# An encoder layer on one core: in each attention step the next head's turned piece moves ahead of the turned probabilities

## Chip, cores and metric

The kernel runs on one core of one Trainium2 chip. The metric is the device time of one execution in microseconds (us).

## What is computed

One encoder layer in float32 for 1024 tokens (prompt) and 256 tokens (sample), which share the weights. The attention of the 8 heads is the part that the change touches:

```
q = norm(c_q) @ w_uq ; kv = norm(c_kv) @ w_ukv          # 8 heads
q, k = norm(q), norm(k), rotary on the last 64 of 192 channels
s = einsum('bqhd,bkhd->bhqk', q, k) * 192**-0.5         # bidirectional
p = softmax(s) ; o = einsum('bhqk,bkhd->bqhd', p, v) ; o @ w_b_out
```

Ahead of it stand the input projection, a gated spatial mixing and its projection; behind it the projection of `o`, the output projection and a layer of 16 experts which each choose their tokens. Every matrix product runs as three products of high and low parts ("hi" and "lo"), to keep float32 precision.

## The kernel before

Five engines run programs of their own, each in its written order, and semaphores tie them together. There are 10 chunks of 128 query tokens, 8 of the prompt (1024 keys) and 2 of the sample (256 keys). The attention stage goes through 80 steps: step n works on head h = n // 10 and on chunk ORD[s], s = n % 10, with ORD = (0, 1, 2, 3, 8, 9, 4, 5, 6, 7). So the steps s = 4 and s = 5 are the small ones. The stage is a pipeline by hand. In step n

- PE (TensorE) issues `scores(n)`, ten matmuls of 512 columns (five of 256 in a small step); `turn_prob(n - 2)`, 8 (or 2) transposes of the probabilities of step n - 2, L1414; one half of `values`, 12 matmuls of 256 columns (3 if the pair of chunks is the small one), L419 to L421, for the pair whose first step is n - 4 or n - 5; and `turn_head`, L1342, 4 or 2 transposes that turn one of nine pieces of the next head's queries and keys out of the token-major tile `tok`. Steps s = 0 to 8 turn one piece each, step s = 9 and head 7 turn none. Pieces 0 to 2 are q, 3 to 5 k, 6 to 8 the rotary parts of both; their sizes are 4, 4 and 2 blocks.
- ACT (ScalarE) does `high(n - 2)` (L2045, pt_hi out of the turned probabilities), `expo(n)` (L2055), at odd n `out_pair` (L2062, which takes the values out of PSUM), and `high_head` (L2011, or L2014 to L2017 for a rotary piece) on the turned piece.
- DVE (VectorE) does `top(n)` (L2540, L2542: the maximum and the bias of the exponential), `low(n - 2)` (L2549, pt_lo), `inverse(n)` (L2555) and `low_head` (L2498, or L2503 and L2505) on the turned piece.
- POOL (GpSimd) scales the probabilities of step n (L984), and in step s = 4 it splits the next head's values (L974, L976).
- SP (SyncE) stores the values and, behind the last turn of a head, loads the queries (L724) and keys (L727) of the head after the next into `tok`.

Pieces of heads 1 to 7 all go through one PSUM bank (`x_bank` gives 7), and the turned probabilities through another pair of banks. What `turn_head` and `turn_prob` wait for:

```
pe.wait_ge(S["q_in"], 16 * (H // 2 + h + 1))
...
free = x - 1 if h == 0 else x
...
if free > 0:
    pe.wait_ge(S["x_hi"], free)
    pe.wait_ge(S["x_lo"], free)
```

```
pe.wait_ge(S["norm_pool"], n + 1)
if n > 0:
    pe.wait_ge(S["pt_lo_dve"], n)
```

`x_hi` counts the pieces whose high part ACT has made, `x_lo` those whose low part DVE has made. A turn of piece x (x counts through all heads) starts when both count x, that is when the piece before has left the bank. `scores(n)` waits for the exponential of step n - 2.

Of the kernel before, what the change touches and what calls it, by code (L numbers as in the profile page):

```python
# [33 lines left out]
H = 8  # L34
# [30 lines left out]
def block_no(p, i):  # L65

    return 8 * (p - 1) + i
# [27 lines left out]
def split_no(g):  # L95

    return g + 1 if g < 2 else g - 1
# [4 lines left out]
PIECES = 9  # L102
# [24 lines left out]
def piece(x):  # L127

    return (0, 2, 1)[x // 3], 4 * (x % 3), (4, 4, 2)[x % 3]
# [26 lines left out]
def build(nc, x_p, x_s, norm1_g, w_in, v_norm_g, w_spatial, b_spatial, w_a_out, q_norm_g, w_uq,  # L156
# [3 lines left out]
    with ctx:  # L160
# [28 lines left out]
        def lin_set(j, b):  # L189
            o = 3 * BANK * j + BLOCKS[b][0]  # L190
            return PS[:, o:o + BLOCKS[b][1]]
# [143 lines left out]
        with ExitStack() as s:  # L335
# [3 lines left out]
            with ExitStack() as s2:  # L339
                sb(s2, "act_room", [P, 2, KD, T])  # L340
                s = s2
# [4 lines left out]
            with ExitStack() as s2:  # L346
                s = s2
# [59 lines left out]
        def at(name, n):  # L407

            return n + credit.get(name, 0)
# [7 lines left out]
        def mm3(pe, out, lh, ll, rh, rl, first, last):  # L417

            pe.matmul(out, lh, rh, start=first, stop=False)  # L419
            pe.matmul(out, lh, rl, start=False, stop=False)  # L420
            return pe.matmul(out, ll, rh, start=False, stop=last)  # L421
# [128 lines left out]
        def x_bank(x):  # L550
            return bank(6 + x % 2 if x < PIECES else 7)
# [544 lines left out]
        def _(pe):  # L1096
# [194 lines left out]
            for p in range(1, PAIRS):  # L1291
                one, other = banks(p)
                for i in range(8):
                    n = block_no(p, i)
# [33 lines left out]
            def turn_head(x):  # L1328

                h, i = divmod(x, PIECES)  # L1330
                kind, c0, cn = piece(i)
                pe.wait_ge(S["q_in"], 16 * (H // 2 + h + 1))
                if kind > 0:
                    pe.wait_ge(S["kv_in"], 16 * (H // 2 + h + 1))
                free = x - 1 if h == 0 else x
                if h == 0:
                    pe.wait_ge(S["pa_copy"], UNITS)
# [3 lines that stand above are left out]
                for c in range(cn):  # L1341
                    last = pe.transpose(x_bank(x)[:, c * P:(c + 1) * P],  # L1342
                                        tok[:, c0 + c, (0, NOPE, HEAD + ROPE)[kind]:][:, 0:P], ident[:])
                last.then_inc(S["x_pe"], 1)
# [39 lines left out]
            def scores(n):  # L1384
                h, s = divmod(n, NCH)
                hd, c = heads[h % 2], ORD[s]
                k0, kn = keys(c)
                if s == 0:
                    if h < 2:
                        pe.wait_ge(S["consts_dve"], 2 * GRP + h + 1)  # L1390
                    pe.wait_ge(S["x_hi"], PIECES * (h + 1))
                    pe.wait_ge(S["x_lo"], PIECES * (h + 1))
                if n > 1:
                    pe.wait_ge(S["exp_act"], n - 1)
                else:
                    pe.wait_ge(S["evac"], 3 * G_B - (3 if n == 0 else 0))
                q = slice(c * P, (c + 1) * P)
                for o in range(0, kn, BANK):
                    w = min(BANK, kn - o)
                    out, k = bank(s_bank(n) + o // BANK, w), slice(k0 + o, k0 + o + w)  # L1400
                    pe.matmul(out, hd["q_hi"][:, q], hd["k_hi"][:, k], start=True, stop=False)  # L1401
                    pe.matmul(out, hd["q_hi"][:, q], hd["k_lo"][:, k], start=False, stop=False)  # L1402
                    pe.matmul(out, hd["q_lo"][:, q], hd["k_hi"][:, k], start=False, stop=False)
                    pe.matmul(out, hd["qr2"][:, q], hd["kr2"][:, k], start=False, stop=False)
                    last = pe.matmul(out, hd["qr2"][:, q], hd["krl"][:, k], start=False, stop=True)  # L1405
                last.then_inc(S["scores_pe"], 1)

            def turn_prob(n):
                kn = keys(ORD[n % NCH])[1]
# [3 lines that stand above are left out]
                for k in range(kn // P):  # L1413
                    last = pe.transpose(bank(4, kn)[:, k * P:(k + 1) * P], prob[:, n % 3, k * P:(k + 1) * P], ident[:])  # L1414
                last.then_inc(S["probT_pe"], 1)

            def values(pr, half):
                h = pr // 5
                hd = heads[h % 2]
                k0, kn = keys(ORD[2 * (pr % 5)])  # L1420
                ks = kn // P // 2
                if half == 0:
                    pe.wait_ge(S["pt_lo_dve"], 2 * pr + 2)
                    if pr % 5 == 0:
                        pe.wait_ge(S["v_lo_pool"], h + 1)
                    if pr > 0:
                        pe.wait_ge(S["values_act"], pr)
                for k in range(half * ks, (half + 1) * ks):
                    v = slice(k0 + k * P, k0 + (k + 1) * P)
                    last = mm3(pe, bank(6, 2 * P), hd["v_hi"][:, v], hd["v_lo"][:, v], pt_hi[:, pr % 2, k],  # L1430
                               pt_lo[:, pr % 2, k], k == 0, k == 2 * ks - 1)
                if half:
                    last.then_inc(S["values_pe"], 1)

            def b_row(j, k, bs=(0, 1, 2)):

                if k == 0:
                    if 0 in bs:
                        pe.wait_ge(S["w_split"], split_no(G_B + j))
                    pe.wait_ge(S["exp_act"], STEPS if 2 in bs else STEPS - 1)  # L1440
                    if j == 1:
                        pe.wait_ge(S["pt_lo_dve"], STEPS)
                if 0 in bs:
                    pe.wait_ge(S["part_lo"], at("part_lo", KD + k + 1))
                for b in bs:
                    t0, tn = BLOCKS[b]
                    last = mm3(pe, lin_set(j, b), w_hi[:, j, k], w_lo[:, j, k], o_hl[:, k, 0, t0:t0 + tn],
                               o_hl[:, k, 1, t0:t0 + tn], k == 0, k == KD - 1)
                    if k == KD - 1:
                        last.then_inc(S["tile_pe"], 1)  # L1450

            for n in range(STEPS + 4):
                h, s = divmod(n, NCH)
                if n < STEPS:
                    scores(n)
                if n == STEPS:
                    for k in range(2):
                        b_row(0, k, (0, 1))
                if 2 <= n < STEPS + 2:
                    turn_prob(n - 2)  # L1460
                if n >= 4:
                    values((n - 4) // 2, n % 2)
                if h < H - 1 and s < PIECES:
                    turn_head(PIECES * (h + 1) + s)
                if n == STEPS:
                    for k in range(2):
                        b_row(0, k, (2,))
                elif STEPS < n < STEPS + 3:
                    b_row(0, n - STEPS + 1)
# [1399 lines left out]
```

## Time and profile before

| | |
|---|---|
| median of 3 runs | 2082.37 us (2081.34 to 2083.27) |
| profiled execution | 2082.28 us, span 2080.6 us |
| PE busy | 2036.2 us, 98% of the span |
| DVE, ACT, POOL busy | 1351.8, 955.2 and 903.4 us |
| mean granted clock of PE | 0.994 |
| attention stage | 713.9 to about 1065 us |

The span runs from the first to the last instruction. Busy times say how long an engine had an instruction in it, and matmuls overlap, so that PE counts as busy through waits that are shorter than the tail of a matmul. The start times in the timeline say more.

### The profile page before, as it was taken

How to read it: one execution, taken by the hardware profiler on the slowest of the kernel's cores; microseconds unless marked ns; L12 is line 12 of the kernel's file. 1: busy time of each engine (PE TensorE's matmuls, PEld its weight loads, DVE VectorE, ACT ScalarE, POOL GpSimd, SP SyncE). 2: the span in 40 equal slices, each digit the busy share in tenths (PEclk: the TensorE clock that was granted, in tenths of full speed). 3: DMA queues.
4: the chain of work that ended last, by engine and by line, in shares of the span. 5: the costliest groups of instructions: out<-in, count | busy, mean ns of one | idle time of the engine just before them, and what ended most of it. 6: DMA issues, size and time to landing. Idle time of an engine off the chain costs nothing.

```text
span 2080.6 us, 33247 instructions
## 1 busy us (share of the span) xinstructions
PE 2036.2 (98%) x13266; PEld 1685.5 (81%) x13266; DVE 1351.8 (65%) x1629; ACT 955.2 (46%) x1188; POOL 903.4 (43%) x640
## 2 busy tenths in 40 slices
PE   8999999999999999999999999799999999999997
PEld 8888888888789888888888877677777777777775
DVE  7864455456767477777655348966777767767774
ACT  8112211113555366666631033456566555655663
POOL 0975555566655376666632601412222322222221
PEclk9999999999999999999999999999999999999999
DMA  4223444333677622232134432588888778888873
GB/s 153 104 104 133 163 166 144 118 92 127 240 234 248 222 64 87 80 104 67 54 112 157 159 142 82 222 343 316 317 308 301 277 276 315 316 316 315 303 286 107
DMA packets 168938, 398.98 MB, mean 192 GB/s; under 512 B 16513, under 2 KB 88193, under 8 KB 168833
## 3 DMA queue, kind: packets, MB, share of 16 engines
q1 hardware_dynamic: 154096, 344.43, 45.2%
q0 software_dynamic: 7680, 20.98, 4.5%
q10 hardware_dynamic: 7056, 32.12, 4.4%
q8 instruction: 72, 1.18, 0.2%
q14 instruction: 34, 0.27, 0.0%
HBM read 318.19 MB, written 79.30 MB: 191 GB/s over the span
## 4 chain that ended last, share of the span: by engine, by line
PE 83%; DVE 10%; ACT 3%; POOL 2%; issue 1%; DMA 1%; SPq 0%; DVEq 0%; POOLq 0%; ACTq 0%
PE PS L1629 25%; PE PS L419 13%; PE PS L420 13%; PE PS L421 13%; PE PS L1660 8%; PE PS L1414 2%; DVE small L2540 2%; DVE topi L2667 1%; DVE topv L2665 1%; DVE work L2669 1%; ACT prob L2055 1%; PE PS L1401 1%; PE PS L1342 1%; PE PS L1405 1%; PE PS L1402 1%
## 5 line engine op out<-in xcount | busy, mean ns | idle before, releaser
L419 PE MATMUL PS<-act_hi,w_hi 128*128 128x256 f32 (+1 forms) x800 | 275.7, 345 | 6.5 <-POOL w_lo L881 2.8
L420 PE MATMUL PS<-act_lo,w_hi 128*128 128x256 f32 (+1 forms) x800 | 270.3, 338 | 0.0
L421 PE MATMUL PS<-act_hi,w_lo 128*128 128x256 f32 (+1 forms) x800 | 269.9, 337 | 0.0
L984 POOL TENSOR_SCALAR prob<-prob,small 128x1024 f32<-128x1024 f32 (+1 forms) x80 | 200.4, 2505 | 120.9 <-DVE small L2555 120.9
L1054 POOL DMA_INDIRECT y_s<-ob_s,ixs_s x16 | 43.9, 2742 | 346.4 <-DVE ob_s L2827 346.4
L2772 DVE TENSOR_TENSOR elo<-raw,ehi 128x2048 fp32r<-128x2048 f32 x65 | 148.7, 2289 | 39.5 <-ACT ehi L2157 39.5
L419 PEld LDWEIGHTS PS<-act_hi,w_hi 128*128 128x128 f32 x800 | 151.9, 190 | 24.1 <-POOL w_lo L881 3.1
L421 PEld LDWEIGHTS PS<-act_hi,w_lo 128*128 128x128 f32 x800 | 151.6, 190 | 16.4
L1629 PE MATMUL PS<-ehi,xT_hi 128*128 128x512 f32 x520 | 164.0, 397 | 0.7 <-DVE xT_lo L2740 0.4
L420 PEld LDWEIGHTS PS<-act_lo,w_hi 128*128 128x128 f32 x800 | 152.0, 190 | 14.7 <-issue 0.7
L1629 PE MATMUL PS<-elo,xT_hi 128*128 128x512 f32 x520 | 160.6, 390 | 0.0
L1629 PE MATMUL PS<-ehi,xT_lo 128*128 128x512 f32 x520 | 160.4, 390 | 0.0
L2157 ACT ACTIVATE ehi<-raw 128x2048 fp32r<-128x2048 f32 x68 | 129.9, 1913 | 63.9 <-PE PS L1629 54.7
L1906 ACT ACTIVATE stg<-stg 128x512 f32<-128x512 f32 x60 | 37.4, 632 | 253.9 <-DVE stg L2321 253.9
L1629 PEld LDWEIGHTS PS<-elo,xT_hi 128*128 128x128 f32 x520 | 97.6, 188 | 20.7
L1629 PEld LDWEIGHTS PS<-ehi,xT_lo 128*128 128x128 f32 x520 | 97.7, 188 | 20.7
L1629 PEld LDWEIGHTS PS<-ehi,xT_hi 128*128 128x128 f32 x520 | 94.7, 188 | 24.0 <-DVE elo L2772 4.4
L2045 ACT ACTIVATE pt_hi<-PS 128x1024 fp32r<-128x1024 f32 (+1 forms) x80 | 71.9, 899 | 87.2 <-PE PS L1414 86.1
L889 POOL TENSOR_TENSOR w_lo<-mix,w_hi 128x512 fp32r<-128x512 f32 x68 | 103.8, 1526 | 5.7
L2772 DVE TENSOR_TENSOR elo<-stg,ehi 128x2048 fp32r<-128x2048 f32 x15 | 34.4, 2292 | 106.6 <-ACT ehi L2157 106.6
L889 POOL TENSOR_TENSOR w_lo<-w_raw,w_hi 128x512 fp32r<-128x512 f32 x72 | 100.7, 1399 | 6.0
L2549 DVE TENSOR_TENSOR pt_lo<-PS,pt_hi 128x1024 fp32r<-128x1024 f32 (+1 forms) x80 | 84.9, 1061 | 27.2 <-ACT pt_hi L2045 27.1
(375 smaller groups left out, 5462.5 us busy)
## 6 DMA issues: line engine op xcount, KB each, us to landing
raw<-in_w_gate SPq DMA_DIRECT2D x64, 1024.0 KB, 8.7
raw_more<-in_w_up SPq DMA_DIRECT2D x32, 1024.0 KB, 12.7
raw_w<-in_w_up SPq DMA_DIRECT2D x32, 1024.0 KB, 16.7
w_raw<-in_w_in SPq DMA_DIRECT2D x16, 1024.0 KB, 7.7
w_raw<-in_w_down SPq DMA_DIRECT2D x15, 1024.0 KB, 6.2
stg<-in_w_down SPq DMA_DIRECT2D x15, 1024.0 KB, 8.6
gt<-in_w_down SPq DMA_DIRECT2D x15, 1024.0 KB, 13.4
raw_end<-in_w_down SPq DMA_DIRECT2D x15, 1024.0 KB, 15.3
```

The costliest lines, as they stand in the source:

```text
L419: pe.matmul(out, lh, rh, start=first, stop=False)
L420: pe.matmul(out, lh, rl, start=False, stop=False)
L421: return pe.matmul(out, ll, rh, start=False, stop=last)
L889: pool.tensor_tensor(ring_lo[:, s], raw_, f32(ring_hi[:, s]), ALU.subtract).then_inc(S["block_lo"], 1)
L984: pool.tensor_scalar(prob[:, n % 3, 0:kn], prob[:, n % 3, 0:kn], prec[:, s:s + 1], None, ALU.mult).then_inc(S["norm_pool"], 1)
L1054: pool.indirect_dma_start(y_quarters, bass.IndirectOffsetOnAxis(ap=ixs_s[:, 0:1], axis=0), ob_s[:], None, compute_op=ALU.add).then_inc(S[" ...
L1629: last = pe.matmul(bank(b0 + half), lhs[:, k], rhs[:, pt, kin, half * BANK:(half + 1) * BANK], start=st, stop=sp_)
L1660: last = pe.matmul(bank(bs)[CAP_S * g:CAP_S * (g + 1), 0:GN], few(k), raws[slot][:, k % 2, g * GN:(g + 1) * GN], start=(k == 0), stop=(k = ...
L2045: act.activation(pt_hi[:, pr % 2, 0:kn // P, o:o + P], bank(4, kn).rearrange("p (k q) -> p k q", q=P), ACT.Copy).then_inc(S["pt_hi_act"], 1)
L2157: act.activation(ehi[:, pt], raws[slot], ACT.Copy).then_inc(S["e_hi"], 1)
L2549: dve.tensor_tensor(pt_lo[:, pr % 2, 0:kn // P, o:o + P], bank(4, kn).rearrange("p (k q) -> p k q", q=P), f32(pt_hi[:, pr % 2, 0:kn // P, ...
L2772: dve.tensor_tensor(elo[:, pt], raws[slot], f32(ehi[:, pt]), ALU.subtract).then_inc(S["e_lo"], 1)
```

## The change

On PE, in each step but the first, `turn_head` moves from the end of the step to the place right behind `scores`, ahead of `turn_prob` and `values`. The programs of the other engines stay as they are.

```
                 if n == STEPS:
                     for k in range(2):
                         b_row(0, k, (0, 1))
+                if n > 0 and h < H - 1 and s < PIECES:
+                    turn_head(PIECES * (h + 1) + s)
                 if 2 <= n < STEPS + 2:
                     turn_prob(n - 2)
                 if n >= 4:
                     values((n - 4) // 2, n % 2)
-                if h < H - 1 and s < PIECES:
-                    turn_head(PIECES * (h + 1) + s)
+                if n == 0:
+                    turn_head(PIECES)
                 if n == STEPS:
                     for k in range(2):
                         b_row(0, k, (2,))
```

## Rows read from the trace of the kernel before

**Rows 1.** The page: busy us, share of the span, instructions

```profile
PE 2036.2 (98%) x13266; PEld 1685.5 (81%) x13266; DVE 1351.8 (65%) x1629; ACT 955.2 (46%) x1188; POOL 903.4 (43%) x640
```

**Rows 2.** Windows, heads 0 and 2: PE, PEld, DVE, ACT, POOL busy; clock, DMA, GB/s

```profile
713.90:753.20 39.30, 36.63 (x228) 31.06 (x227) 27.79 (x49) 25.88 (x44) 24.19 (x11) 1.00 0.33 115
...
796.60:840.10 43.50, 43.32 (x291) 38.65 (x291) 31.50 (x53) 28.95 (x51) 28.77 (x13) 1.00 0.33 100
```

**Rows 3.** Timeline, PE, turned probabilities, steps 20 to 30: start us, length us, idle before

```profile
799.26 1.07 PE L1414 MATMUL PS<-ident,prob 128*128 128x128 f32 x8 [0.17 <-DVE pt_lo L2549]
...
804.35 1.04 PE L1414 MATMUL PS<-ident,prob 128*128 128x128 f32 x8
...
809.40 1.03 PE L1414 MATMUL PS<-ident,prob 128*128 128x128 f32 x8
...
814.21 1.03 PE L1414 MATMUL PS<-ident,prob 128*128 128x128 f32 x8
...
817.71 1.06 PE L1414 MATMUL PS<-ident,prob 128*128 128x128 f32 x8
...
821.24 1.06 PE L1414 MATMUL PS<-ident,prob 128*128 128x128 f32 x8
...
826.12 0.38 PE L1414 MATMUL PS<-ident,prob 128*128 128x128 f32 x2
...
830.50 0.38 PE L1414 MATMUL PS<-ident,prob 128*128 128x128 f32 x2
...
834.89 1.03 PE L1414 MATMUL PS<-ident,prob 128*128 128x128 f32 x8
...
838.80 1.06 PE L1414 MATMUL PS<-ident,prob 128*128 128x128 f32 x8
...
842.79 1.06 PE L1414 MATMUL PS<-ident,prob 128*128 128x128 f32 x8
```

**Rows 4.** Timeline, DVE, pieces of steps 20 to 24, 26, 27; last, pt_lo

```profile
803.19 0.75 DVE L2498 SCALAR_TENSOR_TENSOR q_lo<-PS,small,q_hi 128x512 fp32r<-128x512 f32 x1 [0.42 <-ACT q_hi L2011]
...
808.53 0.75 DVE L2498 SCALAR_TENSOR_TENSOR q_lo<-PS,small,q_hi 128x512 fp32r<-128x512 f32 x1 [0.69 <-ACT q_hi L2011]
...
813.08 0.48 DVE L2498 SCALAR_TENSOR_TENSOR q_lo<-PS,small,q_hi 128x256 fp32r<-128x256 f32 x1 [0.20 <-ACT q_hi L2011]
...
818.38 0.75 DVE L2498 SCALAR_TENSOR_TENSOR k_lo<-PS,small,k_hi 128x512 fp32r<-128x512 f32 x1 [0.69 <-ACT k_hi L2011]
...
821.40 0.75 DVE L2498 SCALAR_TENSOR_TENSOR k_lo<-PS,small,k_hi 128x512 fp32r<-128x512 f32 x1 [0.24 <-ACT k_hi L2011]
...
830.33 0.69 DVE L2505 TENSOR_TENSOR krl<-PS,kr 64x512 fp32r<-64x512 f32 x1
...
835.33 0.69 DVE L2505 TENSOR_TENSOR krl<-PS,kr 64x512 fp32r<-64x512 f32 x1
...
841.43 1.22 DVE L2549 TENSOR_TENSOR pt_lo<-PS,pt_hi 128x1024 fp32r<-128x1024 f32 x1
```

**Rows 5.** Timeline, PE and ACT, step 24: the turn and the high part of its piece

```profile
820.04 0.60 PE L1342 MATMUL PS<-ident,tok 128*128 128x128 f32 x4
...
820.68 0.69 ACT L2011 ACTIVATE k_hi<-PS,small 128x512 fp32r<-128x512 f32 x1 [0.28 <-PE PS L1342]
```

**Rows 6.** Timeline, DVE and PE, head 0: step 1's piece; slots of steps 4 and 10

```profile
723.66 0.75 DVE L2498 SCALAR_TENSOR_TENSOR q_lo<-PS,small,q_hi 128x512 fp32r<-128x512 f32 x1 [0.42 <-ACT q_hi L2011]
...
730.66 0.30 PE L1414 MATMUL PS<-ident,prob 128*128 128x128 f32 x1 [1.29 <-DVE pt_lo L2549]
...
755.74 1.06 PE L1414 MATMUL PS<-ident,prob 128*128 128x128 f32 x8
```

**Rows 7.** The loads of the next queries (line L724)

```profile
DMA to landing us min/median/max: 5.4/5.8/5.9
```

**Rows 8.** Timeline of PE and windows, a wait ahead of the attention stage

```profile
571.29 0.80 PE L419 MATMUL PS<-act_hi,w_hi 128*128 128x512 f32 x1 [2.76 <-POOL w_lo L881]
...
571.00:574.30 3.30, 3.00 (x7) 2.45 (x8) 2.99 (x6) 0.00 (x0) 3.22 (x3) 0.50 0.27 107
```

More of the change, by code:

```diff
@@ L1458, in _ @@
                         b_row(0, k, (0, 1))
+                if n > 0 and h < H - 1 and s < PIECES:
+                    turn_head(PIECES * (h + 1) + s)
                 if 2 <= n < STEPS + 2:
@@ L1462, in _ @@
                     values((n - 4) // 2, n % 2)
-                if h < H - 1 and s < PIECES:
-                    turn_head(PIECES * (h + 1) + s)
+                if n == 0:
+                    turn_head(PIECES)
                 if n == STEPS:
```

## The prediction

> **What bounds the kernel now.** First the busy line of the page: PE has work for 2036.2 us of a span of 2080.6 us [rows 1]. A busy PE can hide waits, so the second view is the table of windows, one window per head of the attention stage. In head 2, and alike in its neighbours, PE is busy for 43.32 of 43.50 us, the other engines for at most 31.50 us [rows 2]. PE's instruction stream is the bound there, and one microsecond that it waits is one microsecond of the kernel, because what follows (the projections) is PE work too. Head 0 is looser: 2.67 us of its 39.30 us are idle [rows 2].
>
> The third view is the timeline of PE, cut down to the first turn of each turned-probability group (L1414) [rows 3]. Its start is the moment at which the scores of the step are issued; I call it the slot, since it is the place into which the change puts the next head's turn. From slot to slot, steps 0 to 9 take 5.09, 5.05, 4.81, 3.50, 3.53, 4.88, 4.38, 4.39, 3.91 and 3.99 us, together 43.53 us. Steps 4 and 5 score queries of the short sequence, which is why the slots behind steps 3 and 4 come early.
>
> The fourth view is the timeline of DVE, cut down to the last use of each turned piece (q_lo, k_lo, krl) [rows 4]. A piece's bank is free when that instruction ends. This is what the moved turn waits for, so everything hangs on how far these ends lie from the slots.
>
> **The change, part by part.** No instruction, byte or semaphore is added or removed. PE's own work stays: turned blocks follow each other every (1.04 - 0.27) / 7 = 0.11 us [rows 3], so four turns cost 0.44 us and two cost 0.22 us on either side of the probabilities. ACT, DVE and POOL keep their programs. What moves is 61 of 63 turns (steps 0 and 1 of head 0 have no probabilities to turn), and with each turn its waits for x_hi and x_lo of the piece before it. These pieces share one bank. Until now those waits stood at the end of the step, behind probabilities and values; now they stand right behind the scores, and turned probabilities, values and the next scores are queued behind them.
>
> When is the previous piece done? In step n ACT does the high part of the turned probabilities, the exponential, at odd steps the copy of the values, and only then the high part of the piece; DVE follows with the low part. So in most steps the chain begins with the turned probabilities of that same step. From the slot to the end of the piece it takes, in steps 0 to 4 [rows 3, 4]: 803.94 - 799.26 = 4.68; 809.28 - 804.35 = 4.93; 813.56 - 809.40 = 4.16; 819.13 - 814.21 = 4.92; 822.15 - 817.71 = 4.44 us. In step 4 ACT stood idle 0.28 us for the turn itself, which PE issued at 820.04 [rows 5]; the new order gives it earlier, which leaves 4.16 us. PE starts about 842.79 - 842.65 = 0.14 us after DVE has freed what it waits for [rows 3, 4].
>
> In the new order this closes a loop: turn (0.44 or 0.22), turned probabilities, ACT, DVE, 0.14 us, next turn. The slot-to-slot time becomes the longer one of the loop and of PE's own time of [rows 3]:
> - Step 0: 0.44 + 4.68 + 0.14 = 5.26 against 5.09.
> - Step 1: 0.44 + 4.93 + 0.14 = 5.51 against 5.05.
> - Step 2: 0.22 + 4.16 + 0.14 = 4.52 against 4.81; 4.81.
> - Step 3: 0.44 + 4.92 + 0.14 = 5.50 against 3.50. The largest term, 2.00 us.
> - Step 4: 0.44 + 4.16 + 0.14 = 4.74 against 3.53, 1.21 us.
> - Step 5: a piece of two blocks as in step 2 with a shorter exponential, so under 4.52 against 4.88; 4.88.
> - Step 6 (rotary piece, three ACT instructions; its exponential waits for the maximum of the scores, not for the turned probabilities): 831.02 - 826.12 + 0.14 = 5.04 against 4.38.
> - Step 7: DVE ends piece to piece 836.02 - 831.02 = 5.00 against 4.39. Before, PE ran ahead of this chain and had it caught up in steps 8 and 9; now it may not.
> - Step 8: the next slot is step 9's, which turns nothing and so waits for no piece; PE's work alone counts: 0.22 + 0.88 + 0.35 + 2.33 = 3.78 against 3.91.
> - Step 9: 0.88 + 0.35 + 2.33 = 3.56 against 3.99, since the next head's first slot now holds a turn whose bank has long been free and which covers the wait for pt_lo (0.17 us at 799.26).
>
> The 0.35 and 2.33 are estimates from step 1's 5.05 us: without its twelve turned blocks (1.32) 3.73 us are left for twelve value products of 256 columns and ten score products of 512; shared out by columns that is 1.40 and 2.33 us, and in steps 8 and 9 a quarter of the value products (0.35) runs. The sum of the ten steps is 48.08 us against 43.53 us: 4.55 us more for each full head, and 6 x 4.55 = 27.3 us for heads 1 to 6.
>
> Head 0: its piece of step 1 ends at 723.66 + 0.75 = 724.41 [rows 6], so the turn of step 2 starts at 724.55. Step 2 adds the loop of 4.52 us (729.07; here the loop is the longer one), steps 3 to 9 the 32.50 us of the list, and head 1's first slot is at 761.57 instead of 755.74 [rows 6]: 5.8 us. Head 7 turns nothing and gains nothing; at its begin no turn covers the wait for pt_lo, which takes the 0.4 us of step 9's gain back once.
>
> 5.8 + 27.3 + 0.4 = 33.5 us. The profiled execution took 2082.28 us (span 2080.6), the median of the runs is 2082.37, so I forecast 2082.3 + 33.5 = 2115.8 us, 1.6% slower.
>
> The moves across the DMA queues cost nothing here: the load of the next queries still waits for the last turn of the head and lands in 5.8 us [rows 7], while the first turn that needs it comes 3.78 + 3.56 = 7.3 us after that turn began. About 1 us of cover is left; were it gone, each head would pay what is missing.
>
> **Rivals.**
> - *The turn fills a gap (other side).* It decides in favour of this if each piece is free 0.14 us before its slot. Then the 0.18 us that PE idles per full head and part of head 0's 2.67 us [rows 2] are filled: some 2 us faster, 2080. For it: in steps 0 and 2 it holds (803.94 before 804.35, 813.56 before 814.21). Against it: step 3's piece ends 819.13, its slot is 817.71; step 4's ends 822.15, its slot 821.24; step 7's ends 836.02, its slot 834.89 [rows 3, 4]. PE would have to pass a turn that waits. 3 in 100; nothing measurable 3 in 100.
> - *Only the short steps count.* If ACT and DVE make up in the long steps what my loops charge there, steps 3 and 4 alone remain: 7 x 3.2 = 22.5 us, 2105. Against it: the loops hang each on the previous turn alone, and nothing in them is slack that a lead could use. 12 in 100.
> - *The clock falls.* Step 3's new wait of 2.0 us is followed by twelve turns. In the trace PE once waited 2.76 us, and the matmuls behind it ran at a granted clock of 0.50, 1.2 GHz [rows 8]; in head 0 a wait of 1.29 us left it at 1.00 [rows 2, 6]. 2.0 us lies between. If it falls once per head, 3.3 us at half speed [rows 8] cost at most 1.65 us: 7 x 1.65 = 11.5 us more, 2128. By the Trainium skill, "TensorE: Matmul & The Clock Gate", section "HAM oscillation — how this bites in real kernels", waits that recur between groups of matmuls do just this, each group paying the ramp again; by that rule the time is this rival's. The trace agrees for 2.76 us and has no wait of 2 us in this stage. 12 in 100.
>
> The forecast itself gets 70 in 100.
>
> **How the numbers follow.** The forecast's own spread comes from the 0.14 us: not under 0.03 (821.37 to 821.40, DVE behind ACT) nor over 0.17 [rows 3 to 5], over 6 waits in each of 7 heads that is -4.6 to +1.3 us; and from the estimates of steps 8 and 9, 0.2 x 7 either way: about 2110 to 2119. The range takes in the rival of the short steps and most of the clock's: 2103 to 2126. A measurement tells about 0.2% (4 us) from no change. Faster 0.03, same 0.03, slower 0.94.
>
> **What the profile of the changed kernel would show.** A head of 48 us instead of 43.5, PE idle 4 to 5 us in it with turns (L1342) as the instruction behind the wait and DVE k_lo, q_lo or krl as what ended it; the longest at the turn of step 4 (2.0 us) and of step 5 (1.2 us), 0.6 us each at steps 7 and 8, none at steps 3, 6 and 0; ACT's wait of 0.28 us for the turn gone; head 7 unchanged. I am wrong if PE shows no idle time before L1342, if a head takes less than 47 or more than 49 us, or if the granted clock in heads 0 to 6 is below 1.00.

## The result and the profile after

The changed kernel takes 2116.66 us (median of 4 runs, 2114.75 to 2117.28) against 2082.32 us, a ratio of 1.0163 with a 95% interval of 1.0151 to 1.0175. It is slower by 34.3 us; forecast were 33.5 us.

The busy line of the page, after:

```profile
PE 2041.5 (97%) x13266; PEld 1687.3 (80%) x13266; DVE 1351.2 (64%) x1629; ACT 955.9 (45%) x1188; POOL 904.7 (43%) x640
```

The counts are those of [rows 1]. The span is 2114.6 us instead of 2080.6 us, and PE's busy time rose by 5.3 us of these 34.0 us; the other 28.7 us are idle time. The windows of heads 0 to 3 show where (columns as in [rows 2]):

```profile
713.90:759.30 45.40, 37.87 (x228) 32.42 (x226) 28.01 (x49) 25.53 (x44) 24.17 (x11) 0.96 0.31 106
759.30:808.30 49.00, 45.24 (x292) 40.04 (x291) 31.44 (x53) 28.90 (x51) 32.16 (x15) 0.97 0.21 68
808.30:856.30 48.00, 43.52 (x292) 38.33 (x291) 31.46 (x53) 28.92 (x51) 28.78 (x13) 1.00 0.29 92
856.30:904.30 48.00, 43.54 (x292) 38.33 (x291) 31.43 (x53) 28.89 (x51) 28.74 (x13) 1.00 0.20 67
```

A full head takes 48.0 us instead of 43.5 us, with the same 43.5 us of PE work in it. Head 0 takes 45.4 us instead of 39.3 us. Head 1 takes 1 us more than the others, at a mean granted clock of 0.97, and its PE work lasts 45.24 us instead of 43.5 us. One window over heads 0 to 6 is 300.30 us long before and 334.60 us after, which is the whole loss:

```profile
713.90:1014.20 300.30, 296.79 (x1968) 263.14 (x1967) 216.81 (x361) 199.64 (x344) 200.20 (x85) 1.00 0.26 83
```

```profile
713.90:1048.50 334.60, 300.94 (x1968) 264.22 (x1967) 216.81 (x361) 199.07 (x344) 200.26 (x85) 0.99 0.23 75
```

The waits of PE in the second of these windows, after (engine, line, what ended the wait; us in total, times, longest):

```profile
PE PS L1342 <- DVE k_lo L2500: 21.4, 13, 3.2
PE PS L1342 <- DVE krl L2507: 6.7, 14, 0.5
PE PS L1342 <- DVE q_lo L2500: 4.6, 8, 1.8
PE PS L1401 <- ACT prob L2057: 0.7, 1, 0.7
```

PE waits 21.4 + 6.7 + 4.6 = 32.7 us, each time at a turn (L1342), and each time DVE's last use of the piece before ends the wait. The waits of turned probabilities are gone; before, there were 2.8 us of them in these heads (last column, idle time):

```profile
L1414 PE MATMUL PS<-ident,prob 128*128 128x128 f32 x460 | 62.1, 274 | 2.8 <-DVE pt_lo L2549 1.8 <-POOL prob L984 0.7
```

So PE's idle time in heads 0 to 6 rose from 3.5 us to 33.7 us, by 30.2 us, and its busy time from 296.8 us to 300.9 us, by 4.1 us. Most of the 4.1 us lie in heads 0 and 1, where the clock fell for a while. Which turns they are is read from the timeline of PE in head 2: the turns of steps 0 to 8, the turned probabilities of step 9, which turns no piece, and the first turn of head 3:

```profile
810.59 0.60 PE L1342 MATMUL PS<-ident,tok 128*128 128x128 f32 x4
...
815.83 0.63 PE L1342 MATMUL PS<-ident,tok 128*128 128x128 f32 x4
...
821.37 0.41 PE L1342 MATMUL PS<-ident,tok 128*128 128x128 f32 x2 [0.32 <-DVE q_lo L2500]
...
826.21 0.60 PE L1342 MATMUL PS<-ident,tok 128*128 128x128 f32 x4
...
831.72 0.63 PE L1342 MATMUL PS<-ident,tok 128*128 128x128 f32 x4 [2.01 <-DVE k_lo L2500]
...
836.41 0.41 PE L1342 MATMUL PS<-ident,tok 128*128 128x128 f32 x2 [1.16 <-DVE k_lo L2500]
...
841.25 0.60 PE L1342 MATMUL PS<-ident,tok 128*128 128x128 f32 x4
...
846.31 0.63 PE L1342 MATMUL PS<-ident,tok 128*128 128x128 f32 x4 [0.51 <-DVE krl L2507]
...
851.32 0.41 PE L1342 MATMUL PS<-ident,tok 128*128 128x128 f32 x2 [0.44 <-DVE krl L2507]
...
855.07 1.06 PE L1414 MATMUL PS<-ident,prob 128*128 128x128 f32 x8
...
858.63 0.60 PE L1342 MATMUL PS<-ident,tok 128*128 128x128 f32 x4
```

These are the slots of steps 20 to 30, to be read against [rows 3]: the step with the longest wait is the small one, step 4, whose scores are over in 0.8 us. What its turn waits for, on DVE, and the high part of its piece on ACT:

```profile
830.82 0.75 DVE L2500 SCALAR_TENSOR_TENSOR k_lo<-PS,small,k_hi 128x512 fp32r<-128x512 f32 x1 [0.69 <-ACT k_hi L2013]
...
834.72 0.69 ACT L2013 ACTIVATE k_hi<-PS,small 128x512 fp32r<-128x512 f32 x1
```

DVE is done with the piece at 831.57 and PE starts the turn at 831.72. ACT no longer stands idle for the turn, as it did for 0.28 us in [rows 5]; it comes to it late, behind turned probabilities and exponential, while the turned piece lies in its bank from 832.35 to 834.72.

### The profile page after: what moved, and what is told of

Its sections match the earlier page's. It is cut to its first block, busy times and chain, and to the rows that moved or that the text cites. A ratio compares the mean times of both kernels' runs of the same rounds, so it can differ in the third digit from the quotient of the medians.

```text
span 2114.6 us, 33247 instructions
## 1 busy us (share of the span) xinstructions
PE 2041.5 (97%) x13266; PEld 1687.3 (80%) x13266; DVE 1351.2 (64%) x1629; ACT 955.9 (45%) x1188; POOL 904.7 (43%) x640
## 4 chain that ended last, share of the span: by engine, by line
PE 82%; DVE 10%; ACT 4%; issue 2%; POOL 2%; DMA 0%; SPq 0%; POOLq 0%; DVEq 0%; ACTq 0%
PE PS L1631 24%; PE PS L419 12%; PE PS L420 12%; PE PS L421 12%; PE PS L1662 8%; PE PS L1414 3%; ACT prob L2057 1%; PE PS L1342 1%; DVE topi L2669 1%; DVE topv L2667 1%; DVE work L2671 1%; DVE small L2542 1%; PE PS L1401 1%; PE PS L1405 1%; PE PS L1402 1%
## 5 line engine op out<-in xcount | busy, mean ns | idle before, releaser
L2774 DVE TENSOR_TENSOR elo<-raw,ehi 128x2048 fp32r<-128x2048 f32 x65 | 148.8, 2290 | 39.3 <-ACT ehi L2159 39.2
L887 POOL TENSOR_SCALAR w_hi<-w_raw 128x512 fp32r<-128x512 f32 x72 | 54.9, 762 | 111.8 <-PE PS L421 111.6
```

Source lines behind the costliest of these rows:

```text
L2774: dve.tensor_tensor(elo[:, pt], raws[slot], f32(ehi[:, pt]), ALU.subtract).then_inc(S["e_lo"], 1)
```

## The experiments

All changes are given against the changed kernel, all times against the kernel before on the same chip, 2082.1 to 2082.7 us. The theory is the loop of the prediction. Its first rival is an even price: every moved turn delays ACT's chain by its own length, so each of the 61 moves would cost the same.

**Steps 4 and 5 alone.**

```
-                if n > 0 and h < H - 1 and s < PIECES:
+                if n > 0 and h < H - 1 and s < PIECES and s in (4, 5):
...
-                if n == 0:
-                    turn_head(PIECES)
+                if n == 0 or h < H - 1 and s < PIECES and s not in (4, 5):
+                    turn_head(PIECES * (h + 1) + s)
```

> The turn moves ahead in steps 4 and 5 of each head alone (14 of the 61 moves). Theory of the loop (a moved turn waits until the piece before it has left the one bank): the turn of step 4 waits about 1.5 us, as DVE ends the piece of step 3 at 819.13 and the slot is 817.71, and the turn of step 5 about 1.2 us; 7 heads x 2.7 us = 19 us, 2101.4 us. Rival of the even price (each moved turn delays ACT by its own length, so each move costs 34.3 / 61 = 0.56 us): 14 x 0.56 = 8 us, 2090 us.

Measured: 2102.93 us, ratio 1.0100 (1.0083 to 1.0117), 20.2 us more. The moves in two of the nine steps make 59% of the loss, which the even price can't. The two waits, timeline of PE, head 4:

```profile
918.91 0.63 PE L1342 MATMUL PS<-ident,tok 128*128 128x128 f32 x4 [1.56 <-DVE k_lo L2500]
...
923.59 0.41 PE L1342 MATMUL PS<-ident,tok 128*128 128x128 f32 x2 [1.16 <-DVE k_lo L2500]
```

Heads 1 to 6 pay 2.7 us each, as the loop says. The 1.2 us above its 19 us are about what the clock cost in head 0: behind a wait of 2.85 us it stayed down for 6 us, and from this turn to the next it took 738.76 - 732.60 = 6.16 us, where it takes 923.59 - 918.91 = 4.68 us in head 4:

```profile
732.60 1.09 PE L1342 MATMUL PS<-ident,tok 128*128 128x128 f32 x4 [2.85 <-DVE k_lo L2500]
```

```profile
732.60:738.70 6.10, 6.10 (x29) 6.10 (x30) 2.34 (x5) 2.15 (x4) 2.45 (x2) 0.50 0.01 3
```

**All steps but 4 and 5.** The same edit with `s not in (4, 5)` ahead and `s in (4, 5)` behind.

> The turn moves ahead in all steps but 4 and 5 (47 of the 61 moves). Loop: the waits of steps 1, 2, 7 and 8 stay (0.2, 0.5, 0.65, 0.5 us) and head 0 pays about 3 us, 14 us in all, 2096.6 us; with the run of steps 4 and 5 alone it adds up to the whole loss. Even price: 47 x 0.56 = 26 us, 2109 us.

Measured: 2098.09 us, ratio 1.0073 (1.0056 to 1.0090), 15.4 us more; 47 of the 61 moves cost less than the 14 others. 20.2 + 15.4 = 35.6 us against 34.3 us for the whole: the parts add up, within their intervals.

**Steps 0, 3 and 6 alone.** The same edit with `s in (0, 3, 6)`.

> The turn moves ahead in steps 0, 3 and 6 alone (20 of the 61 moves), where the piece before has left the bank ahead of the slot. Loop: no wait in heads 1 to 6, some 0.1 us per head and 1.3 us in head 0, 2084 us at most. Even price: 20 x 0.56 = 11 us, 2093.5 us.

Measured: 2085.84 us, ratio 1.0016 (1.0008 to 1.0025), 3.4 us more, twice the 1.7 us that the loop gave it at most, and a third of the even price. The profiled execution, from which the rows are, took 2087.05 us. Windows of head 0, of 3.4 us within it, of heads 3 and 4:

```profile
714.00:756.10 42.10, 37.98 (x229) 32.62 (x227) 27.88 (x49) 25.77 (x44) 24.21 (x11) 0.96 0.31 108
732.50:735.90 3.40, 3.40 (x18) 3.40 (x17) 2.22 (x4) 1.63 (x4) 2.61 (x1) 0.50 0.00 0
843.40:887.00 43.60, 43.16 (x292) 38.75 (x291) 31.53 (x53) 28.99 (x51) 28.80 (x13) 1.00 0.22 74
887.00:931.90 44.90, 43.45 (x292) 38.71 (x291) 31.56 (x53) 29.02 (x51) 28.82 (x13) 1.00 0.23 75
```

The plain heads take 43.6 us, as expected. The rest is in head 0 (2.8 us instead of 1.3 us) and in head 4. In head 0 the clock fell behind a wait of 1.87 us, and step 4 takes 737.13 - 732.20 = 4.93 us from slot to slot instead of 3.53 us in the kernel before: these are 1.4 us. The run before it (all steps but 4 and 5) has a wait of the same length at the same place and keeps its clock at 1.00. The two waits, this run's first:

```profile
732.20 1.69 PE L1414 MATMUL PS<-ident,prob 128*128 128x128 f32 x8 [1.87 <-DVE pt_lo L2551]
```

```profile
734.77 1.06 PE L1414 MATMUL PS<-ident,prob 128*128 128x128 f32 x8 [1.87 <-DVE pt_lo L2551]
```

In head 4 the first turn, which now stands right behind the scores, met a wait for the load of its queries:

```profile
890.55 0.66 PE L1342 MATMUL PS<-ident,tok 128*128 128x128 f32 x4 [1.00 <-DMA tok<-q_d]
```

```profile
DMA to landing us min/median/max: 5.4/5.8/7.0
```

The second fence is the answer for the line of these loads (L724): one of them took 7.0 us instead of 5.8 us. This is the cover of which the prediction found about 1 us; in this run there is less of it, since the last turn of a head still stands at the end of step 8 and the load is issued behind it: at 883.48, only 6.1 us ahead of the moment at which the turn could have started (890.55 - 1.00).

**The turn in the middle.** Scores, turned probabilities, turn, values.

```
-                if n > 0 and h < H - 1 and s < PIECES:
-                    turn_head(PIECES * (h + 1) + s)
                 if 2 <= n < STEPS + 2:
                     turn_prob(n - 2)
+                if n > 0 and h < H - 1 and s < PIECES:
+                    turn_head(PIECES * (h + 1) + s)
```

> Each turn stands between the turned probabilities and the values. The turned probabilities no longer wait behind it, and each piece has 0.87 us more to leave its bank. Loop: waits stay at the turns of step 4 (0.65 us) and step 7 (0.4 us) alone, 5 us in all, 2087.4 us. Rival (what counts is that the turn stands ahead of the values and the next scores, wherever exactly): at least half of the loss stays, 2099 us or more.

Measured: 2085.49 us, ratio 1.0017 (1.0007 to 1.0027), 3.5 us more by the ratio and 2.8 us by the medians. The waits that stay are those of steps 4 and 7, here in head 4:

```profile
908.59 0.63 PE L1342 MATMUL PS<-ident,tok 128*128 128x128 f32 x4 [0.50 <-DVE k_lo L2500]
...
920.96 0.63 PE L1342 MATMUL PS<-ident,tok 128*128 128x128 f32 x4 [0.28 <-DVE krl L2507]
```

So 0.87 us (eight turned blocks) more for each piece, and an ACT chain that isn't delayed by the turn, take away nine tenths of the loss; the run doesn't part the two. It is the place ahead of the turned probabilities, and hardly that ahead of values and scores, that costs.

**Another bank for two pieces.**

```
-            return bank(6 + x % 2 if x < PIECES else 7)
+            return bank(6 + x % 2 if x < PIECES else {4: 1, 5: 3}.get(x % PIECES, 7))
...
-                free = x - 1 if h == 0 else x
+                free = x - 1 if h == 0 else {4: 0, 5: 0, 6: x - 2}.get(i, x)
...
+                if h < H - 1 and s in (6, 7):
+                    pe.wait_ge(S["x_hi"], PIECES * (h + 1) + s - 1)
+                    pe.wait_ge(S["x_lo"], PIECES * (h + 1) + s - 1)
                 if n > 1:
                     pe.wait_ge(S["exp_act"], n - 1)
```

> The changed kernel, with the pieces of steps 4 and 5 in banks 1 and 3, the halves of the score banks that the small scores of these steps leave empty; their turns wait for no piece, the turn of step 6 for that of step 3, and the scores of steps 6 and 7 wait until those pieces are out. Loop: the waits of 2.0 and 1.2 us go, those of steps 1, 2, 7 and 8 stay, 21 us of the loss come back, 2095 us. Rival (ACT and DVE can't do the work sooner, whatever the bank): the wait comes back at the next scores or turned probabilities, 2112 us or more.

Measured: 2095.30 us, ratio 1.0064 (1.0047 to 1.0081), 12.6 us more: 21.7 us of the 34.3 us come back. PE's order is that of the changed kernel, every turn stands ahead of the turned probabilities; what two of the nine turns wait for is gone, the turn of step 6 waits for the piece of step 3, and the scores of steps 6 and 7 have waits of their own for the two pieces. The timeline of PE in head 4, steps 2 to 5:

```profile
905.03 0.41 PE L1342 MATMUL PS<-ident,tok 128*128 128x128 f32 x2 [0.30 <-DVE q_lo L2503]
...
909.88 0.60 PE L1342 MATMUL PS<-ident,tok 128*128 128x128 f32 x4
...
913.23 0.60 PE L1342 MATMUL PS<-ident,tok 128*128 128x128 f32 x4
...
916.75 0.38 PE L1342 MATMUL PS<-ident,tok 128*128 128x128 f32 x2
917.36 0.30 PE L1417 MATMUL PS<-ident,prob 128*128 128x128 f32 x1 [0.22 <-DVE pt_lo L2554]
```

The wait of step 2 stands, those of steps 4 and 5 are gone; 0.22 us turn up at the turned probabilities of step 5. Over the whole stage waits of this kind are 3.7 us in ten places.

**The piece first on ACT and DVE.** PE as in the changed kernel; in each step ACT begins with the turned piece, and DVE takes it right behind the maximum.

```
+                if h < H - 1 and s < PIECES and n > 0:
+                    high_head(PIECES * (h + 1) + s)
                 if 2 <= n < STEPS + 2:
                     high(n - 2)
...
-                if h < H - 1 and s < PIECES and n > 0:
-                    high_head(PIECES * (h + 1) + s)
...
                 if n < STEPS:
                     top(n)
+                if h < H - 1 and s < PIECES and n > 0:
+                    low_head(PIECES * (h + 1) + s)
                 if n > 1:
                     low(n - 2)
...
-                if h < H - 1 and s < PIECES and n > 0:
-                    low_head(PIECES * (h + 1) + s)
```

> PE as in the changed kernel, but ACT takes the high part of the turned piece first in each step and DVE its low part right behind the maximum. Loop: the piece leaves its bank in the same step long before the next slot, no turn waits, and the time is that of the kernel before, 2081 us; a head takes 43.6 us. Rival (even price, or PE's order itself): it stays above 2110 us. A third way: the exponential comes late behind the piece and the loss moves there, 2090 us or more.

Measured: 2081.28 us, ratio 0.9993 (0.9984 to 1.0002). The whole loss is gone with PE's program untouched. Step 3 of head 4 in the timelines of PE, ACT and DVE, and the turn of step 4 behind it:

```profile
899.03 0.60 PE L1342 MATMUL PS<-ident,tok 128*128 128x128 f32 x4
...
899.66 0.69 ACT L2013 ACTIVATE k_hi<-PS,small 128x512 fp32r<-128x512 f32 x1 [1.96 <-PE PS L1342]
900.61 0.74 DVE L2500 SCALAR_TENSOR_TENSOR k_lo<-PS,small,k_hi 128x512 fp32r<-128x512 f32 x1
902.36 0.60 PE L1342 MATMUL PS<-ident,tok 128*128 128x128 f32 x4
```

From turn to the end of the piece it takes 901.35 - 899.03 = 2.32 us. In the changed kernel the piece of step 3 (in head 2) takes 831.57 - 826.21 = 5.36 us. In the whole stage one turn still waits for a piece, 0.4 us in head 0, and the turned probabilities wait 4.5 us in 17 places (2.5 us in 6 in the kernel before). Head 2 takes 840.64 - 797.17 = 43.47 us from its first slot to head 3's, as before.

**The piece first in steps 0, 6 and 7.** The moves on PE, ACT and DVE in these steps; the other steps as in the kernel before.

> As the run with the piece first, but in steps 0, 6 and 7 alone; all other steps as in the kernel before. Loop: the turn fills the waits for pt_lo at steps 8, 9 and 0 (0.3 us per head) and part of head 0's idle time, 3 to 4 us faster than the kernel before, 2079 us. Rival (these gaps are not worth anything, as other waits stand behind them): 2082.3 us.

Measured: 2078.41 us, ratio 0.9979 (0.9970 to 0.9988), 4.1 us faster by the medians than the kernel before, and the fastest of all that were run. The window of head 2 has no idle time of PE left:

```profile
795.90:838.70 42.80, 42.79 (x292) 38.72 (x291) 31.77 (x53) 29.20 (x50) 28.73 (x13) 1.00 0.33 100
```

The cover of the load is thin here too: the first turn of head 4, at 884.48, waited 0.17 us for a load that was issued at 878.51. The new order of ACT and DVE in these three steps was not run without PE's moves, nor PE's moves without it, so how the 4.1 us divide between them isn't shown.

**Head 0 in the old order.**

```
-                if n > 0 and h < H - 1 and s < PIECES:
+                if n >= NCH and h < H - 1 and s < PIECES:
...
-                if n == 0:
-                    turn_head(PIECES)
+                if n < NCH and s < PIECES:
+                    turn_head(PIECES + s)
```

> The changed kernel with head 0 in the old order, so 54 of the 61 moves. Loop: head 0 goes back to 39.3 us from 45.4 us and heads 1 to 6 keep their 48.0 us, 2116.7 - 6.1 = 2110.6 us; if the clock does not fall in head 1 either, that head takes 48.0 instead of 49.0 us and the time is 2109.6 us. Rival (the waits of 2.0 us at step 4 are what brings the clock down in the changed kernel, and which of the six it is, is chance): a head of 48.9 us shows somewhere among heads 1 to 6. Even price: 54 x 0.56 = 30 us, 2112.6 us.

Measured: 2109.07 us, ratio 1.0127 (1.0110 to 1.0144), 7.6 us less than the changed kernel by the medians. The profiled execution took 2111.86 us, the slowest of the four. Windows of heads 0, 1 and 2:

```profile
715.70:755.00 39.30, 36.67 (x228) 31.05 (x226) 27.77 (x49) 25.87 (x44) 24.18 (x11) 1.00 0.33 114
755.00:804.00 49.00, 45.26 (x292) 40.06 (x292) 31.46 (x53) 28.84 (x51) 32.20 (x15) 0.97 0.24 77
804.00:852.00 48.00, 43.52 (x292) 38.32 (x291) 31.41 (x53) 28.83 (x51) 28.76 (x13) 1.00 0.29 91
```

Head 0 is back at 39.3 us, and heads 1 and 2 take what they take in the changed kernel, the fall of the clock in head 1 included. So head 1's fall doesn't hang on head 0's. The mean clock of the four executions was 0.992 (the profiled one), 0.991, 0.994 and 0.994, and the last two took 2108.24 and 2107.44 us, the shortest times; that these two went without the fall in head 1 would fit, but only the first has a profile.

## Why the prediction was right

**The bound.** PE's stream sets the stage; this held. All of the loss lies in heads 0 to 6 (334.60 - 300.30 = 34.3 us). Waits at turns bring 32.7 us, the old waits of the turned probabilities take 2.8 us off, and 4.1 us are PE work that took longer, most of it in the two heads where the clock fell.

**The loop, step by step.** From slot to slot in head 2 the changed kernel takes 5.24, 5.54, 4.84, 5.51, 4.69, 4.84, 5.06, 5.01, 3.75 and 3.56 us. Forecast were 5.26, 5.51, 4.81, 5.50, 4.74, 4.88, 5.04, 5.00, 3.78 and 3.56 us. No step is off by more than 0.05 us, and the sum is 48.04 us against 48.08 us. This is because a moved turn starts the loop anew: its terms are durations of the old trace that the change doesn't touch. The run with the piece first shows the loop as cause from ACT's and DVE's side, the run with other banks from the side of the place, the run in the middle that of the distance between them.

**Head 0** was forecast to put head 1's first slot at 761.57; it is at 761.70. That it fits so well is in part luck: step 3 took 734.40 - 729.14 = 5.26 us instead of 5.50 us, and step 4, with the clock down, 739.33 - 734.40 = 4.93 us instead of 4.74 us. The 0.8 us by which the whole forecast is short are about what the fall in head 1 cost.

**The exit to head 7** was priced at 0.4 us and cost about 0.3 us: the step 9 ahead of it takes 1051.12 - 1047.30 = 3.82 us instead of 3.56 us.

**The DMA's cover** (about 1 us) was as computed: in the changed kernel the load is issued at 851.75, 6.9 us ahead of the turn at 858.63, and these loads take 5.6 to 6.2 us there. No turn waits for one. The run of steps 0, 3 and 6 showed how thin that cover is.

**The rivals.** The turn that fills a gap is real but small. In the changed kernel steps 8 and 9 are 0.16 and 0.43 us shorter than before, as the prediction had it, and it may be part of the 4.1 us of the run in steps 0, 6 and 7, where ACT and DVE take the piece early. With their order as it was, no run came out faster. That only the short steps count is out: the others cost 15.4 us. The fall of the clock, held for the less likely, did occur, in heads 0 and 1, once each:

```profile
735.50:738.90 3.40, 3.40 (x18) 3.40 (x17) 1.66 (x3) 2.15 (x4) 0.79 (x2) 0.50 0.02 5
783.30:786.70 3.40, 3.40 (x18) 3.40 (x17) 0.41 (x1) 1.47 (x4) 0.88 (x1) 0.50 0.00 0
```

```profile
734.40 0.63 PE L1342 MATMUL PS<-ident,tok 128*128 128x128 f32 x4 [3.17 <-DVE k_lo L2500]
...
782.83 0.66 PE L1342 MATMUL PS<-ident,tok 128*128 128x128 f32 x4 [2.01 <-DVE k_lo L2500]
```

Ahead of the first stands a wait of 3.17 us, ahead of the second one of 2.01 us; both times it ran at 1.2 GHz for 3.4 us. Heads 2 to 6 have the same wait of 2.0 us at the same turn and stay at 2.4 GHz. So a wait of 2 us can be followed by a fall and mostly is not. By the prediction's own sign (the granted clock in heads 0 to 6 below 1.00) it would have been wrong here; the sign was too strict, since the price is small. In head 1 step 4 takes 788.38 - 782.83 = 5.55 us instead of 4.69 us, 0.9 us more, and in head 0 4.93 us, 0.2 us more. That is less than the 1.65 us that I gave it at most, since the slower stretch ran in part into step 5's wait, which in head 1 is 0.43 us instead of 1.16 us. Where no wait stands behind it to take it in, it costs more: 1.4 us in the run of steps 0, 3 and 6. (The prediction's sum for this rival, 2115.8 + 11.5, is 2127.3 us, not 2128.)

```profile
788.38 0.42 PE L1342 MATMUL PS<-ident,tok 128*128 128x128 f32 x2 [0.43 <-DVE k_lo L2500]
```

By the Trainium skill ("TensorE: Matmul & The Clock Gate", section "HAM oscillation — how this bites in real kernels") recurring waits each pay for a fall; its case has waits of some 3 to 5 us for a DMA. The trace agrees in head 0 (3.17 us). For the waits of 2.0 us, shorter than those of the page, it shows one fall in six.

What stays open: why the clock falls in head 1 and not in the five heads that look the same, in the changed kernel and in the run without head 0, and why a wait of 1.87 us is followed by a fall in one run and not in the other. No run varied the length of a wait alone, or moved the stage in time.

## What to carry to other kernels

A work item that is moved forward on one engine brings its waits with it, and everything behind it in that engine's order pays for them. Before moving it, put the end of what it waits for beside its new place, step by step, in a trace of the old order: the small steps, where the new place comes early, decide. With a single buffer the move forward cost 34 us as long as the consumers kept their order, and nothing once they followed in all steps. Moved in three steps alone, with the consumers following in these, it gained 4 us.

## What the runs showed of the hardware

The load of a head's queries landed in 5.8 us in the median, and once, with the same bytes, in 7.0 us (before: 5.4 to 5.9 us [rows 7]). In that run the turn could have started 6.1 us after the issue, and it waited 1.0 us; against such a load the 6.9 us of the changed kernel would fall 0.1 us short.

After a wait of 2.0 us at the same turn PE's clock fell to 1.2 GHz for 3.4 us in one head and not in five others. After a wait of 1.87 us at the same turned probabilities of head 0 it fell in one run and not in another. What one fall of 3.4 us cost went from 0.2 and 0.9 us, where a wait behind it took part of it in, to 1.4 us, where none did.
